# Residual parts of the expert weights in smaller instructions, and GpSimd's share of them at the head of its slot, in a one-core decoder layer

## The reference

```python
def one(xc):
    qh = (xc @ w_query).astype(jnp.float32).reshape(chunk, PEER_HEADS, D_KEY)
    s1 = jnp.einsum('nhk,hmk->nhm', qh[..., :HALF_KEY], keys1.astype(jnp.float32))
    s2 = jnp.einsum('nhk,hmk->nhm', qh[..., HALF_KEY:], keys2.astype(jnp.float32))
    v1, i1 = lax.top_k(s1, PEER_TOPK)
    v2, i2 = lax.top_k(s2, PEER_TOPK)
    ...
    top, pos = lax.top_k(cand, PEER_TOPK)
    idx = jnp.take_along_axis(cidx, pos, axis=-1)
    g = jax.nn.softmax(top, axis=-1).astype(xc.dtype)
    act = jax.nn.gelu(jnp.einsum('nd,nhkd->nhk', xc, expert_u[idx]), approximate=False)
    return jnp.einsum('nhk,nhkd->nd', g * act, expert_v[idx])
```

## Time and profile before

| | |
|---|---|
| time, median of 3 runs (lowest to highest) | 2011.5 us (2010.46 to 2014.94) |
| time of the profiled execution | 2014.13 us |
| its span in the trace | 2012.6 us |
| busy share of the span: PE, DVE, ACT, POOL | 92%, 74%, 41%, 58% |
| mean granted TensorE clock | 0.961 |
| moved to and from HBM | 243 GB/s over the span |

### The profile page before, as it was taken

The page is one execution under the profiler, slowest core; times in us unless marked ns, Lnnn a source line. Parts: engine busy times, 40 slices in busy tenths (PEclk is TensorE's granted clock), DMA queues, the critical chain, the costliest instruction groups (busy, mean ns, idle before and its releaser), DMA issues.

```text
span 2012.6 us, 37912 instructions
## 1 busy us (share of the span) xinstructions
PE 1851.2 (92%) x14571; PEld 1738.0 (86%) x14571; DVE 1482.0 (74%) x2584; ACT 820.0 (41%) x1103; POOL 1158.1 (58%) x855
## 2 busy tenths in 40 slices
PE   6988988788999999999998988989998999998898
PEld 6977764357999999999997988989998998998898
DVE  3669665522589889857774878888877888888887
ACT  4233664422223545447774333333333343433332
POOL 3223222223225888864556776777777777777761
PEclk9989998889999999999998999999999999999999
DMA  5333877662124777766687988889998898989885
GB/s 164 79 108 136 285 256 268 228 256 84 57 92 130 232 226 222 233 204 229 247 332 253 310 302 313 305 300 320 326 323 304 311 329 303 316 316 313 296 283 189
DMA packets 207789, 492.19 MB, mean 245 GB/s; under 512 B 34209, under 2 KB 119266, under 8 KB 187138
## 3 DMA queue, kind: packets, MB, share of 16 engines
q1 hardware_dynamic: 145906, 319.11, 46.9%
q0 software_dynamic: 55296, 167.94, 22.9%
q10 hardware_dynamic: 6416, 2.78, 1.0%
HBM read 449.10 MB, written 40.66 MB: 243 GB/s over the span
## 4 chain that ended last, share of the span: by engine, by line
PE 65%; DVE 12%; POOL 6%; another core or an unknown queue 5%; ACT 4%; issue 4%; DVEq 2%; DMA 1%; SPq 0%; ACTq 0%; POOLq 0%
PE pair L1529 18%; PE pair L1531 17%; PE pair L1530 17%; PE pair L1862 3%; PE pair L1674 3%; POOL v_rows L658 2%; DVE pair L1428 2%; POOL picked_a L651 2%; DVE act L1470 2%; POOL w_lo L646 1%; PE pair L1686 1%; DVE w_lo L1485 1%; DVE x_lo L1485 1%; PE pair L1726 1%
## 5 line engine op out<-in xcount | busy, mean ns | idle before, releaser
L1529 PE MATMUL pair<-x_hi,w_hi 128*128 128x256 f32 (+2 forms) x2224 | 662.9, 298 | 45.3 <-POOL w_lo L646 22.6
L1530 PE MATMUL pair<-x_lo,w_hi 128*128 128x256 f32 (+2 forms) x2224 | 651.8, 293 | 0.1
L1531 PE MATMUL pair<-x_hi,w_lo 128*128 128x256 f32 (+2 forms) x2224 | 650.9, 293 | 0.0
L1529 PEld LDWEIGHTS pair<-x_hi,w_hi 128*128 128x128 f32 x2224 | 432.7, 195 | 52.9 <-POOL w_lo L646 27.9
L1530 PEld LDWEIGHTS pair<-x_lo,w_hi 128*128 128x128 f32 x2224 | 432.3, 194 | 0.5 <-issue 0.3
L1531 PEld LDWEIGHTS pair<-x_hi,w_lo 128*128 128x128 f32 x2224 | 430.2, 193 | 0.0
L658 POOL DMA_INDIRECT v_rows<-in_v_t,at_row x256 | 305.7, 1194 | 171.7 <-DVE pair L1428 103.1
L1428 DVE SCALAR_TENSOR_TENSOR pair<-v_rows,share,pair 128x1024 f32<-128x1024 f32 x254 | 327.5, 1289 | 25.0 <-issue 2.7
L651 POOL DMA_INDIRECT picked_a<-acts_sparse,at_unit x256 | 274.9, 1074 | 80.3 <-issue 74.9
L646 POOL TENSOR_TENSOR w_lo<-w_raw,w_hi 128x1024 fp32r<-128x1024 f32 x106 | 251.4, 2395 | 90.5 <-ACT w_hi L924 90.3
L954 ACT ACTIVATE act<-pair 128x288 f32<-128x288 f32 x128 | 52.4, 410 | 527.4 <-PE pair L1531 263.4
(11 more groups left out here) (234 smaller groups left out, 3712.3 us busy)
## 6 DMA issues: line engine op xcount, KB each, us to landing
w_raw<-in_u_t SPq DMA_DIRECT2D x74, 1024.0 KB, 5.3
v_raw<-in_u_t SPq DMA_DIRECT2D x54, 1024.0 KB
w_raw<-in_v_t SPq DMA_DIRECT2D x128, 256.0 KB
v_raw<-in_v_t SPq DMA_DIRECT2D x128, 256.0 KB
gates<-g_out SPq DMA_DIRECT2D x9, 2048.0 KB, 9.2
g_in<-gates SPq DMA_DIRECT2D x16, 1152.0 KB
v_ring<-in_cache_v SPq DMA_DIRECT2D x64, 256.0 KB, 4.3
v_ring<-in_cache_v POOLq DMA_DIRECT2D x64, 256.0 KB, 4.6
```

Source lines behind the costliest of these rows:

```text
L1529: te.matmul(out, s_hi, m_hi, start=start, stop=False)
L1530: te.matmul(out, s_hi, m_lo, start=False, stop=False)
L1531: return te.matmul(out, s_lo, m_hi, start=False, stop=stop)
```

## The change

Three edits, all to subtractions that make low parts:

1. `split_u` on GpSimd: each half of 128x1024 becomes two instructions of 128x512. The signal of a half is on the second. This holds for both stages.
2. `split_u` and `split_v` on VectorE: one instruction of 128x2048 becomes four of 128x512, the signal on the last.
3. GpSimd's order in a slot of the second stage: its `split_u` stands ahead of all of the slot's fetches, and not between the two halves of them.

```diff
                 for j in range(2):
                     cols = slice(P * j, P * (j + 1))
-                    pool.tensor_tensor(lows[w][:, :, cols], by_blocks(u_raw[u_buffer(t)])[:, :, cols],
-                                       highs[w][:, :, cols].bitcast(F32), ALU.subtract).then_inc(u_lo_pool, 1)
+                    for first in (0, KD // 2):
+                        mine = slice(first, first + KD // 2)
+                        last = pool.tensor_tensor(lows[w][:, mine, cols], by_blocks(u_raw[u_buffer(t)])[:, mine, cols],
+                                                  highs[w][:, mine, cols].bitcast(F32), ALU.subtract)
+                    last.then_inc(u_lo_pool, 1)
...
-                mine = rows_added_at(slot)
-                for k in mine[:len(mine) // 2]:
-                    fetch_ahead(k)
                 if slot + 1 < STEPS and not on_vector(STEPS + slot + 1):
                     split_u(STEPS + slot + 1)
-                for k in mine[len(mine) // 2:]:
+                for k in rows_added_at(slot):
                     fetch_ahead(k)
...
-                v.tensor_tensor(lows[w], by_blocks(u_raw[u_buffer(t)]), highs[w].bitcast(F32), ALU.subtract)\
-                    .then_inc(u_lo_vector, 2)
+                for q in range(4):
+                    mine = slice(2 * q, 2 * q + 2)
+                    last = v.tensor_tensor(lows[w][:, mine], by_blocks(u_raw[u_buffer(t)])[:, mine],
+                                           highs[w][:, mine].bitcast(F32), ALU.subtract)
+                last.then_inc(u_lo_vector, 2)
...
-                v.tensor_tensor(lows[w], by_blocks(v_raw[c % 2]), highs[w].bitcast(F32),
-                                ALU.subtract).then_inc(v_lo_done, 1)
+                for q in range(4):
+                    mine = slice(2 * q, 2 * q + 2)
+                    last = v.tensor_tensor(lows[w][:, mine], by_blocks(v_raw[c % 2])[:, mine],
+                                           highs[w][:, mine].bitcast(F32), ALU.subtract)
+                last.then_inc(v_lo_done, 1)
```

## The result

The changed kernel took 2117.9 us (median of 4 runs, 2112.89 to 2127.15) beside 2013.2 us for the kernel before: ratio 1.0514, 95% interval [1.046, 1.0569]. The forecast was 1930, its range 1906 to 1974. Yet the same program, unchanged, took 2108 us in a later group of runs and 1941 us in another, on a chip other than that of the later group, where its ratio is 0.9617 [0.9601, 0.9633]. The kernel before took 2010 to 2020 us beside each. So there are two questions: where did the time go, and what differs between the chips.

A forecast was written before the change was run, and what follows sets the result against it. TensorE was taken to bound the second stage, stalled 5.5 us a period by GpSimd's late subtraction. 19.3 x (43.77 - 39.5) = 82 us off the 2011.5 median, first stage nothing, gave 1930 us; range 1906 to 1974.

The forecast's parts named there:

- What bounds the kernel now: Second stage: TensorE stalls for GpSimd's late subtraction, 104 us in all; the late gelu was taken as a consequence.
- Rival B: Second stage: the late gelu has its own cause, TensorE waits for VectorE's V part instead; 2009 us, chance 0.06.
- the sum: Second stage: 19.3 periods shortened from 43.77 to 39.5 us, 82 us off; first stage nothing; median 1930 us.
- the 5.5 us in every period: Second stage: each period of three slots was read as 5.5 us too long, 43.77 where TensorE needs 38.3.
- Edit 3, the order: GpSimd's second-stage slot: subtraction starts 5.0 us sooner, which alone could nearly close the 5.5 us stall a period.
- rival A: Second stage: GpSimd becomes the bound as fetches don't get between quarters; period 41.6 us, 1969 us, chance 0.20.
- Edit 2, VectorE's quarters: VectorE's subtractions: cost +1.0 us a period, hidden behind TensorE; GpSimd's fetches save half of 4.9 us a period.
- my term of +0.2: VectorE: four subtractions of 512 elements take 2.41 us, +0.2 us for each subtraction split.
- Edit 1, GpSimd's quarters: GpSimd's subtraction: VectorE's gate multiply waits at most 1.3 us; gain up to 1 us a period, cost 0.2.
- What is late next: Second stage: TensorE, VectorE, GpSimd and DMA then need nearly the same time, within 3%; period 39.5 us.
- Rival C: Second stage: rows land late and stop VectorE at `add_row`, up to 4.9 us a period; 2031 us, chance 0.08.

The follow-up runs named there:

- e13: All three edits on the kernel before, run again unchanged on another chip, one without held gelus: 1940.86 us, ratio 0.9617.
- e17: Only GpSimd's subtraction moved ahead of its slot's fetches, against the kernel before, on a chip without held gelus: 1971.62 us, ratio 0.9766.
- e6: GpSimd's subtraction in pieces of 512 and moved ahead of the fetches, VectorE's whole, against the kernel before: 1977.6 us, ratio 0.9811.
- e2: Smaller subtractions on both GpSimd and VectorE, GpSimd's order as before, against the kernel before: 2074.65 us, ratio 1.0296.
- e9: All three edits on the kernel before, run again unchanged on a chip with held gelus: 2108.24 us, ratio 1.0459.
- e18: VectorE's quarters and GpSimd's new order, against the kernel before, on the same chip as e17: 1934.63 us, ratio 0.9595.
- e3: Only VectorE's low parts in four instructions, GpSimd's as before, against the kernel before: 2074.24 us, ratio 1.0286.
- e14: VectorE's quarters and GpSimd's new order, against the kernel before, on the same chip as e13: 1935.65 us, ratio 0.9595.
- e12: VectorE's quarters and GpSimd's new order, with one pair of fetches between GpSimd's two subtraction halves, against the kernel before: 2055.8 us, ratio 1.0228.
- e1: Only GpSimd's subtraction moved ahead of its slot's fetches, against the kernel before, on a chip with held gelus: 1962.87 us, ratio 0.9743.
- e4: The changed kernel without gelu-value fetches, the share multiplied by itself instead; against the kernel before 1920.82 us, ratio 0.9527.
- e7: VectorE's quarters and GpSimd's new order, GpSimd's subtraction in two pieces as before, against the kernel before: 1936.93 us, ratio 0.9592.
- e15: GpSimd's subtraction in pieces of 512 and moved ahead of the fetches, against the kernel before, same chip as e13: 1974.81 us, ratio 0.9787.
- e11: Only GpSimd's subtraction moved ahead of its slot's fetches, against the kernel before, same chip as e9: 1959.11 us, ratio 0.9743.

## Why the prediction was wrong, point by point

**The step that failed** stands in "What bounds the kernel now": "I can't say from the trace why that gelu waits; its time moves with the subtraction, and I take it as a consequence of TensorE being blocked." The gelu was held by something that has no releaser in the trace, and it moved with the subtraction, most likely because the subtraction ended a run of fetches. Rival B had named a cause of its own, at chance 0.06, and priced it as no change, by way of waits for VectorE's V part; those are 15.9 us here, and what came was TensorE's 99.6 us without a releaser. What the sum lacked is a term for what edit 2's shorter fetches do to the other engines where gelus are held. With all three edits that turned -82 us into +105 and +98 (2117.9 - 2013.2 and 2108.24 - 2010.51), and TensorE, busy or idle, needs 166.4 us more in 19 periods than in e13. On the three free chips there is no hold, and the forecast's time came out.

A second step failed with it: the prediction took the stall of the earlier trace rows, 5.00 us for GpSimd, as the place of the 5.5 us in every period. The same trace, 1115 to 1900 us, had only 16.0 us of that in 11 waits, and more without a releaser:

```profile
PE pair L1529 <- POOL w_lo L646: 16.0, 11, 5.0
...
PE pair L1529 <- issue: 11.8, 20, 1.5
...
PE pair L1531 <- issue: 11.0, 20, 1.2
...
PE pair L1530 <- issue: 6.6, 13, 0.8
```

On a free chip the wait for GpSimd may well be the larger part (e17 and e6 still have 21.1 and 28.4 us of it); that isn't shown for the kernel before. So the hit there, 1941 for 1930 us, is in part luck: its 5.5 us were read from a trace in which the hold was at work.

**"Edit 3, the order"** held in part. With edit 2 beside it, TensorE's waits for GpSimd fell to 1.0 us in all. Alone it gave 48 to 52 us on three chips, not nearly all of 104, since GpSimd then has no time left (in e17 TensorE still waits for it, up to 5.1 us): rival A's load, with a period of 41.6 and 1969 us worked out, and 41.2 to 41.8 and 1959 to 1972 measured. On holding chips it doesn't add up with the other edits: on top of edits 1 and 2 it took the ratio from 1.030 (e2) to 1.046 (e9, on another chip).

**"Edit 2, VectorE's quarters"**: the cost was right, 2.50 us for four against 2.29. The trace agrees with my term of +0.2. It doesn't bear out the Trainium skill's "VectorE: DVE Perf Modes" (section on the TRN2 errata), whose latency for each instruction would by my estimate have made it 2.8 us. The Trainium skill's "SBUF — State Buffer" (section "Who interferes with whom") infers that a two-input instruction on VectorE leaves GpSimd's descriptor writing alone; a fetch as a whole was lengthened by it all the same, as the times that follow show. They don't tell which part of a fetch was held, since it also reads its indices (`at_row`) from SBUF, so my reading that the inference fails went too far. The gain was put too low. With edit 3, on one free chip (e17 and e18), fetches fell from 1240 + 1173 to 991 + 968 ns, 0.45 us a pair or 5.6 us a period at 12.4 pairs, where I took 2.5 of at most 4.9. But I priced it only on GpSimd: what denser fetches do to the other engines had no term. On a holding chip edit 2 costs 59 us alone (e3).

**"Edit 1, GpSimd's quarters"** was priced at up to 1 us a period gained on VectorE, 0.2 lost on GpSimd, and nothing in the first stage. It measured +5 us (e13 beside e14, with intervals that overlap) on a free chip and nothing on a holding one without edit 3 (e2 beside e3, 0.4 us); with edit 3 it may have a part in the 52 us between e12 and e9. Its mechanism was wrong. Pieces in a row don't let VectorE in after 1.3 us. In e13:

```profile
1307.70 5.73 DVE L1473 TENSOR_TENSOR act<-act,g_in 128x288 f32<-128x288 f32 x2
1307.73 5.01 POOL L648 TENSOR_TENSOR w_lo<-w_raw,w_hi 128x512 fp32r<-128x512 f32 x4
```

Two multiplies that elsewhere take 0.82 us waited through all four pieces. With the two pieces of 1024 in e18 the same pair took 5.44. TensorE's last waits on a free chip are for VectorE's V part (12.9 + 6.5 us in e13, 11.1 + 6.5 in e18), which stands behind those gates; that the gates cause them fits but isn't shown.

**"What is late next" and the sum** held on free chips. A period was to be 39.5 us and was 40.3 (e13) and 39.9 (e18: 758.88 / 19). The DMA share was to be 0.97 and was 0.95 and 0.96. The forecast's 82 us off compare with 2019.35 - 1940.86 = 78.5. The first stage was nothing, as said: TensorE busy for 448.33 of 456 us.

**Rival C**, the only one on the slower side, did not happen: adds wait for 0.4 us in all. The slower outcome came from a mechanism that wasn't on the list with that sign.

**What stays open.** Whether holding belongs to the chip itself or to a state that lasted for a group isn't told: each group ran on its own chip. The kernel before has no trace from a free chip. What holds TensorE's issue and its signal to ScalarE isn't named by any row. That the loss takes a holding chip, VectorE's quarters and all of the fetches together is shown by e3 and e12 against e1, e4 and e7. That the density of the fetches is the link is argued, from the timing of the long holds; whether it would be the making of the fetches on GpSimd or the full DMA queues that they lead to (share 1.05 in the stall) wasn't separated either, since e4 lowers both and its trace isn't used. Nor is VectorE's order of work in quarters excluded as a part of it. Exactly edits 2 and 3 never ran on a holding chip, so edit 1's part in the result isn't separated.

## What to carry to other kernels

A wait for which the trace names no releaser is a cause that you don't know yet; don't fold it into the wait beside it. Ask what would happen to it if the change succeeds, and give that a price on the slower side. Before one stall in a timeline is taken for all periods, add up its kind of wait over the whole stage. When an engine gets faster at starting transfers, ask what the denser transfers may do to the others, not only what the engine gains. And time a change that lives on such margins on several chips: here edit 3 alone gives 2.3 to 2.6% on all three where it ran, edits 2 and 3 give 4% on three, while the variant of them in e12 loses 2% and all three edits lose 5% on others. Unless the chip is known, edit 3 alone is the one to keep.

## What the runs showed of the hardware that I had not expected

- One program, unchanged, took 2118 and 2108 us in two groups and 1941 on another chip, while the kernel that it came from took 2010 to 2020 beside all of them. On free chips even the waits repeat across chips: e14 and e18 both have 410.5 us in 107 gelu waits, e6 and e15 447.4 and 448.2 in 103. On holding chips they don't (e1 and e11: 148.4 in 20 and 142.3 in 17; the kernel before: 192.0 in 18 and 158.2 in 15).
- On a holding chip TensorE, with no wait that the trace names, started matmuls 0.7 to 1.4 us apart during a run of indirect fetches, and a gelu started 7 us after the last matmul that it needs (1373.38 to 1380.56).
- Four subtractions of 512 elements in a row on GpSimd keep VectorE's two-input multiplies out as two of 1024 do, to the last one's end: 5.73 and 5.44 us for two multiplies that elsewhere take 0.82. But with four such pieces on VectorE a fetch of GpSimd's takes 0.99 and 0.97 us on average (e18), where with whole ones of 2048 it takes 1.17 and 1.24 (e17).
